# Other orders in an attention and a delta stage, and 20 transposes of the identity ahead of each head's inverse

## The reference, cut to what matters

```python
u = rmsnorm(x); p = u @ W_in                      # one projection, split by columns
o_A = neighbourhood_attention(p)                  # 8 heads of 64, a relative-position bias
o_B = gated_deltanet(p)                           # 4 heads of 128, forward and backward
o_C = rglru(p)
x = x + W_out(sum_b sigmoid(G_b(u)) * (o_b @ W_br[b]))
x = x + relu(rmsnorm(x) @ W1)**2 @ W2

# neighbourhood attention, for a block of queries and its window of keys
s = where(col_ok, q @ k.T / 8 + bias, -inf); o = softmax(s) @ v

# delta rule, for one head and direction, g summed up within a chunk
decay = exp(g_i - g_j)                            # i >= j; below strict: i > j
a_mat = (k * beta) @ k.T * strict * decay
u, w  = solve(I + a_mat, [v * beta, k * beta * exp(g)])
for each chunk:
    v_new = u - w @ S
    o = (q * exp(g)) @ S + (q @ k.T * decay) @ v_new
    S = S * exp(g_last) + (k * exp(g_last - g)).T @ v_new
o = rmsnorm(o_fwd + o_bwd) * norm_w * silu(z)
```

## Time and profile before

| | us |
|---|---|
| median of 3 runs (lowest to highest) | 3051.58 (3047.43 to 3055.48) |
| the profiled execution's own time | 3052.57 |
| span of that execution | 3050.9 |
| busy in it: PE | 2883.6 |
| DVE, ACT, POOL | 1299.3, 1072.3, 1204.7 |

### The profile page before, as it was taken

The page is one execution under the profiler, slowest core; times in us unless marked ns, Lnnn a source line. Parts: engine busy times, 40 slices in busy tenths (PEclk is TensorE's granted clock), DMA queues, the critical chain, the costliest instruction groups (busy, mean ns, idle before and its releaser), DMA issues. The chain is left out here.

```text
span 3050.9 us, 38569 instructions
## 1 busy us (share of the span) xinstructions
PE 2883.6 (95%) x15219; PEld 2351.4 (77%) x15219; DVE 1299.3 (43%) x1953; ACT 1072.3 (35%) x1829; POOL 1204.7 (39%) x805
## 2 busy tenths in 40 slices
PE   6999999999999969588778999999999999999998
PEld 5878787877888846477667887878888888888887
DVE  5233233221479959666664352322233232232323
ACT  4241313243044539455543122332332323233232
POOL 2222122121123320433422423466666676756663
PEclk9999999999999979778899999999999999999999
DMA  4434233343545357210113545332323333333331
GB/s 115 169 131 139 80 102 102 100 128 98 177 155 168 129 190 250 79 53 22 74 47 119 172 155 201 99 111 86 108 85 95 97 97 124 99 95 96 114 108 56
DMA packets 239572, 352.78 MB, mean 116 GB/s; under 512 B 32929, under 2 KB 186273, under 8 KB 239393
## 3 DMA queue, kind: packets, MB, share of 16 engines
q1 hardware_dynamic: 239392, 350.32, 35.3%
HBM read 263.71 MB, written 96.36 MB: 118 GB/s over the span
## 5 line engine op out<-in xcount | busy, mean ns | idle before, releaser
L102 PE MATMUL pj_acc<-u_hi,pj_w_hi 128*128 128x512 f32 x1464 | 576.4, 394 | 10.6 <-DVE u_lo L823 10.6
L2774 DVE TENSOR_TENSOR x_tm<-m_ps,x_tm 128x512 f32<-128x512 f32 x384 | 265.0, 691 | 744.2 <-PE m_ps L104 744.2
L104 PE MATMUL pj_acc<-u_hi,pj_w_lo 128*128 128x512 f32 x1464 | 571.8, 391 | 0.0
L103 PE MATMUL pj_acc<-u_lo,pj_w_hi 128*128 128x512 f32 x1464 | 571.2, 390 | 0.0
L551 POOL TENSOR_TENSOR pj_w_lo<-pj_w_raw,pj_w_hi 128x1024 fp32r<-128x1024 f32 x61 | 159.3, 2612 | 721.6 <-ACT pj_w_hi L600 721.6
L2656 POOL TENSOR_TENSOR m_lo<-gate,held 128x1024 fp32r<-128x1024 f32 x96 | 237.9, 2501 | 269.8 <-ACT held L2573 269.8
L102 PEld LDWEIGHTS pj_acc<-u_hi,pj_w_hi 128*128 128x128 f32 x1464 | 275.8, 188 | 85.6 <-issue 18.2
L104 PEld LDWEIGHTS pj_acc<-u_hi,pj_w_lo 128*128 128x128 f32 x1464 | 275.8, 188 | 58.2
L103 PEld LDWEIGHTS pj_acc<-u_lo,pj_w_hi 128*128 128x128 f32 x1464 | 276.1, 189 | 56.2
L102 PE MATMUL m_ps<-held 128*128 128x512 f32 x768 | 298.9, 389 | 2.4 <-DVEq L2755 2.4
L102 PE MATMUL m_ps<-held,m_h_hi 128*128 128x512 f32 x768 | 299.5, 390 | 0.0
(11 more groups left out here) (308 smaller groups left out, 4930.9 us busy)
## 6 DMA issues: line engine op xcount, KB each, us to landing
gate<-in_w_mlp_dram SPq DMA_DIRECT2D x48, 1024.0 KB, 5.4
gate<-in_w_mlp_dram SPq DMA_DIRECT2D x96, 512.0 KB, 3.7
proj<-pj_stage SPq DMA_DIRECT2D x61, 768.0 KB, 3.4
pj_w_raw<-in_w_in_dram SPq DMA_DIRECT2D x61, 512.0 KB, 5.2
gate<-proj SPq DMA_DIRECT2D x24, 768.0 KB, 4.4
mo_w_raw<-in_w_out_dram SPq DMA_DIRECT2D x48, 256.0 KB, 2.9
rpb_bias<-pj_shut SPq DMA_DIRECT2D x48, 192.0 KB, 3.0
rpb_bias<-rpb_near SPq DMA_DIRECT2D x24, 384.0 KB
```

The lines of the kernel that those rows point to most:

```text
L102: pe.matmul(out, w_hi, x_hi, start=first, stop=False)
L103: pe.matmul(out, w_hi, x_lo, start=False, stop=False)
L104: return pe.matmul(out, w_lo, x_hi, start=False, stop=last)
L2774: dve.tensor_tensor(xt, ps2[:, q % 4], xt, ALU.add).then_inc(added, 1)
```

## The change

It has these parts. Tile names are those of the code.

- Attention: SP issues bias tables 4, 5 and 6 ahead of pair 1, whose loads go in two halves at units 4 and 6; the decay rows come at unit 8 and not at 1. The columns of head 0 are not made here. Instead DVE forms -g and ln(beta) + g for all heads with two operations ahead of the loop and one in unit 6, and ACT takes the logarithm first. The 48 exponentials start at unit 14.
- Delta, arithmetic: beta goes into the exponent of the strict decays, so that `scores` is one operation of 128x512 instead of four of 128x128. The columns (`cx`) of all heads are made once, at the start, with two matmuls, eight small DVE operations and one exponential; they are gone from the inverses.
- Delta, places: the exponentials of the decay rows go from steps 0 and 2 of the inverse to steps 5 and 6 of the chunk phase before it. `cut_blocks` stands behind the state updates of its step. ACT takes over four of the copies into `dn_un`, and the inverse waits for the parts of it singly. The sum of the output stage comes behind the first U copy, its 24 length matmuls are three groups of 8 at steps 3, 4 and 5, the root at step 8 (was 5), the gate at step 15 (was 12). POOL multiplies the queries in six pieces of 512.
- Before each inverse PE transposes the identity 20 times into a PSUM bank that is free at that point.

The diff, cut to its core:

```diff
 # attention
-    DG_AT, DCOL_AT, DY_AT, DEXP_AT = 1, 6, (28, 32, 36), 8
+    DG_AT, PAIR1_AT, DCOL_AT, DY_AT, DEXP_AT = 8, (4, 6), 6, (28, 32, 36), 14
             load_bias(3)
-            for a in range(2):
-                load_qk(1, a)
-                load_v(1, a)
             for u in range(U + 4):
...
                 if n is not None:
                     load_bias(n)
+                if u in PAIR1_AT:
+                    load_qk(1, PAIR1_AT.index(u))
+                    load_v(1, PAIR1_AT.index(u))
...
                 if u == DCOL_AT:
-                    decay_columns(dve, dc, cols[:, 0], col2[:, 0], ncol2[:, 0], cx2[:, 0], gq[:, 0])
+                    dve.tensor_tensor(gbeta[:], cols[:, :, 0:2], gbeta[:], ALU.add).then_inc(d_cols, 1)
...
 # delta
-SQUARES_AT, ROOT_AT, EG_AT, CEXP_AT = 1, 5, (0, 2), 10
-LENGTHS_AT, MEAN_AT, DIAG_AT, SPREAD_AT, NORM_AT, GATE_AT = 2, 3, 5, (7, 9, 11), (8, 10, 12), 12
+SUM_AT, SQUARES_AT, LENGTHS_AT, MEAN_AT, ROOT_AT, DIAG_AT = 0, 2, (3, 4, 5), 6, 8, 8
+SPREAD_AT, NORM_AT, GATE_AT = (10, 12, 14), (11, 13, 15), 15
-COLUMNS_AT = 6
-INCL_AT = {8: 4, 11: 5, 13: 0, 15: 1}
+INCL_AT = {9: 4, 12: 5, 15: 0}
-INCL_END = {1: 3, 3: 2}
+INCL_END = {1: 1, 3: 3, 4: 2}
+WARM = 20
+EG_IN = (5, 6)
...
             def place(i):
+                for q in Q32:
+                    act.copy(by_direction(un, q, 0)[:, 0:NTB:2, :, q], compact(c1, q, 0)[:, 0:NTB:2]).then_inc(S["un0_d0"], 1)
+                act.wait_ge(S["spread"], 2 * i + 2)
...
                 pe.wait_ge(S["am_done"], i * NG6 + NG6)
                 pe.wait_ge(S["qk_done"], i * NG6 + NG6)
+                for j in range(WARM):
+                    pe.transpose(ps[:, 7, j % 4], ident[:], ident[:])
...
-                for j in range(4):
-                    last = dve.scalar_tensor_tensor(am[:, n, j], ps[:, 4 + 2 * (GRAMS.index(tg) % 2), j],
-                                                    ncol2[:, i % 2, 2 + d, 4 * tg + j:4 * tg + j + 1], decays[:, j], ALU.mult, ALU.mult)
-                last.then_inc(S["am_done"], 1)
+                dve.scalar_tensor_tensor(am[:, n], ps[:, 4 + 2 * (GRAMS.index(tg) % 2)], -1.0, decays, ALU.mult,
+                                         ALU.mult).then_inc(S["am_done"], 1)
...
-                if part == CUT_IN:
-                    cut_blocks(i)
...
+                if more and step == CUT_IN:
+                    cut_blocks(i + 1)
```

More of the change, by code:

```diff
@@ L1701, in _ @@
             act.wait_ge(mixed_landed, 16)
-            act.sem_inc(S["cexp"], 1)
             act.sem_inc(S["exp_s"], NG6)
             act.sem_inc(S["exp_i"], NG6)
+            act.wait_ge(S["columns"], 5)
+            flat_cx = cx[:].rearrange("p h a t -> p (h a t)")
+            act.activation(flat_cx, flat_cx, ACT.Exp).then_inc(S["cexp"], 1)
+            for d in range(2):
+                row_decays(0, d)
             cut_blocks(0)
@@ L1836, in main @@
                         pe.matmul(o, nb[:, j], qk2[:, i % 2, 2 * (t // 4) + d, t % 4], start=step == 0, stop=True).then_inc(S["o_mm"], 1)
+            pe.wait_ge(S["ends"], 2)
+            for d in range(2):
+                last = pe.matmul(ps[:, 3, d, 0:HEADS * NT], work[:, d * P:(d + 1) * P], cols[:, :, d], start=True, stop=True)
+            last.then_inc(S["ends"], 1)
             for x in range(NTB):
@@ L1869, in out_gate, with columns, rates @@
                 dve.scalar_tensor_tensor(oc[0], oc[0], 0.5, zt, ALU.mult, ALU.mult).then_inc(S["out_done"], 1)
[L1871 to L1875 removed]
+            def columns():
+                c = Chain(dve, S["columns"], 0, 5)
+                c.add(dve.tensor_copy(cx[:, :, 0:2], cols[:, :, 0:2]))
+                dve.wait_ge(S["ends"], 3)
+                for d in range(2):
+                    ends = ps[:, 3, d, 0:HEADS * NT].rearrange("p (h t) -> p h t", h=HEADS)
+                    c.add(dve.tensor_tensor(cx[:, :, 2 + d], ends, cols[:, :, d], ALU.subtract))
+                    c.add(dve.tensor_copy(cx[:, :, 4 + d], ends))
+                c.end()
+            def rates():
+                dve.wait_ge(S["cexp"], 1)
+                dve.scalar_tensor_tensor(cx[:, :, 0:2], cols[:, :, 2:4], -1.0, cx[:, :, 0:2], ALU.mult, ALU.mult).then_inc(S["columns"], 1)
+                dve.wait_ge(S["columns"], 6)
             def scores(i, n):
[L1879 removed]
+                tg = UN[n][0]
                 decays = am[:, n] if i else dd0[:, 2 * n]
@@ L1984, in main @@
                             out_gate(i - 1)
-                    if k == COLUMNS_AT and more:
-                        columns(i + 1, nxt)
                 dve.sem_inc(S["s0"], 1)
@@ L2005, in main @@
                         if step:
-                            dve.scalar_tensor_tensor(st[:, j], st[:, j], cx2[:, i % 2, EGL[d], t:t + 1], ps[:, j, 2], ALU.mult, ALU.add).then_inc(S["st_ev"], 1)
+                            dve.scalar_tensor_tensor(st[:, j], st[:, j], cx[:, i, EGL[d], t:t + 1], ps[:, j, 2], ALU.mult, ALU.add).then_inc(S["st_ev"], 1)
                         else:
                             dve.tensor_copy(st[:, j], ps[:, j, 2]).then_inc(S["st_ev"], 1)
+                    if more and step == CUT_IN:
+                        cut_blocks(i + 1)
                 if more:
-                    place(i + 1, False)
-                c.end()
+                    place(i + 1)
             dve.wait_ge(S["prm_in"], 16)
-            chains = [Chain(dve, S["chain"], i, K_DN) for i in range(HEADS)]
+            for d, row in ((0, P - 1), (1, 0)):
+                dve.tensor_copy(work[:, d * P:(d + 1) * P], ident[:, row:row + 1].to_broadcast([P, P])).then_inc(S["ends"], 1)
             dve.memset(ps[:, 0:2], 0.0).then_inc(S["blank"], 1)
-            dve.sem_inc(S["chain"], 8)
-            chains[0].n = 8
-            dve.sem_inc(S["cols_in"], 1)
-            for part in range(STEPS):
-                prepare(0, part, chains[0])
-            place(0, False)
+            for step in range(STEPS):
+                prepare(0, step)
+                if step == 0:
+                    columns()
+                if step == CUT_IN:
+                    cut_blocks(0)
+                if step == WIDE_IN:
+                    rates()
+            place(0)
             for i in range(HEADS - 1):
-                main(i, True, chains[i], chains[i + 1])
-            main(HEADS - 1, False, chains[HEADS - 1], None)
+                main(i, True)
+            main(HEADS - 1, False)
             dve.wait_ge(S["gated"], HEADS)
@@ L2039 @@
                 K_KEPT.append((_step, _j))
-K_DN = 1 + 7 + 1
 class MlpViews:
```

148 lines of the change are left out of this document (64 added, 84 removed).

## The result

| | before | after |
|---|---|---|
| median of 4 runs (lowest to highest), us | 3051.58 (3047.43 to 3055.48) | 3029.19 (3025.76 to 3031.12) |
| ratio, 95% interval | | 0.9924 (0.9909 to 0.9940) |
| the profiled execution's own time, its span | 3052.57, 3050.9 | 3031.12, 3029.1 |

The kernel is 22.4 us faster, where 46.6 were forecast: the sign was right and the size half. The stages tell where the rest went. The attention runs from its first score product to the start of its last product with the values, an inverse begins with its first product S, a chunk phase with its first product with `dn_un` (L1821), and what follows head 3 with the 24 length matmuls of the merge (L2355). The times are read off the two timelines of PE; the low time is worked out from the granted clock as in the prediction.

A forecast was written before the change was run, and what follows sets the result against it. The inverses, one dependent chain over PE, ACT and DVE with PE often at low clock, were taken as the bound, with waits in the attention. Terms summed to -46.9 us from 3052.6, giving 3005 for the median; range 2984 to 3034.

The forecast's parts named there:

- Start of the inverses: Start of each inverse: ACT shares copies, the sum comes later, row exponentials leave; -3.3 for heads 1 to 3, -1.5 head 0, -11.4.
- Other work inside: Inside the inverses: split lengths -4.5, columns gone less closer table loads -3.4, later gate -2.0 us.
- Chunk phases: Chunk phases: shorter scores, cut moved and earlier POOL solution, less row exponentials on ACT; -1.8 for each of three, -5.4 us.
- What bounds the kernel: Inverses are one PE, ACT, DVE chain; 92 us at low clock, at best 33 shorter (36%) at full clock.
- Attention: Attention: bias wait gone -7.9, column operations replaced -6.2, contention +2.5, exponentials over fewer units +0.5; sum -11.1 us.
- The upper figure of 15 us: Attention: by the port-lock rule, scalings beside twelve POOL masks could pay up to 15 us; the rows gave 2.5.
- Head 0's preparation: Preparation of head 0: wider scores operations -2.3, new columns work +1.2; sum -1.1 us.
- Head 0's inverse: Inverse of head 0: forecast 4.4 us shorter.
- The clock in the second halves: Second halves of the inverses: less stalling keeps the clock up longer; -5 us, bounds 0 and -20.
- rival 5: Inverses: back-to-back table loads at steps 8 and 9 drop the clock, kernel slower at 3058 us; chance 0.06.
- The transposes: Ahead of the inverses: 20 transposes keep PE from idling; -1.0 for each of three heads, -3 us; 0 to +6 by the rule.
- rival 2: Delta stages: gains hidden by POOL and ACT's fuller queue, row exponentials cost +3 a head; 3031 us, chance 0.13.

The follow-up runs named there:

- earlier_output: Also number 12: number 11 with the output stage early again (mean at step 4, root 6, spread, norm and gate pieces from 8 to 14): 3003.2 us.
- number 7: The changed kernel with SP's load order of before in the attention (pair 1 ahead of bias tables 4 to 6, decay rows at unit 1): 3029.7 us.
- numbers 8: The changed kernel with all 24 length matmuls at step 3 instead of in three groups: 3024.1 us.
- 16: earlier_output with the length matmuls in three groups at steps 3, 4, 5, the mean at 5 and the diagonal at 7: 3000.5 us.
- number 11: The changed kernel with the column matmuls behind the first Gram product, all lengths at step 3, and the gate in three pieces at steps 12, 14, 15: 3018.7 us.
- gate_pieces: The changed kernel with the gate as three pieces of 512 columns at steps 12, 14 and 15: 3025.2 us.
- number 9: The changed kernel with the decay-row exponentials of heads 1 to 3 back at steps 0 and 2 of the inverse: 3021.1 us.
- 10: The changed kernel with DVE's cut ahead of the state updates of step 2, as before: 3022.2 us.
- number 3: The kernel before with the 20 transposes, and POOL waiting for DVE's 16 copies before it multiplies the queries: 3051.8 us.
- 15: earlier_output with DVE's cut ahead of the state updates of step 2: 3004.0 us.

## Why the prediction was half right

The steps that failed are the prices of the moved work in its new places: in "Start of the inverses" the sum, in "Other work inside" the lengths and the gate (-6.5 together), and "Chunk phases" (-5.4). With the clock they were to bring most of the 28.8 us; the inverses of heads 1 to 3 gave 2.1 us, and the chunk phases became 6.9 us longer. Head 0's two stages were off by 5 us and 7 us in opposite directions.

**What bounds the kernel.** Right: the inverses are one chain over three engines, a stall stands ahead of many falls of the clock (not of all, see below), and the low time in them was there to be had. earlier_output took 40 of the 64 low us of heads 1 to 3, and its 3003 us are the time that was forecast for the change.

**Attention.** Right, -11.9 against -11.1. The bias wait went (number 7 brings 6.7 of it back) and the columns with it. Contention was under-sized: five pairs of scalings were slowed by 6.8 us together, against 2.5 in two pairs before, thus by 4.3 more and not by 2.5. The better clock (low 26 to 11 us) is what can have made up for that; no run separates it. The upper figure of 15 us that the prediction names wasn't reached.

**Head 0's preparation.** Wrong by 5 us. "The new `columns` work adds +1.2" counted the short DVE operations. The cost was in the queue of PE: its matmuls for the columns stand ahead of the Gram products and wait 6.5 us for two DVE copies, which themselves wait for the stage's first DMA. The scores were as forecast, 0.65 us each.

**Head 0's inverse.** -11.8 against -4.4. It has no output stage. With the columns' wait of 3.1 us gone and no row exponentials ahead of the S copies, PE's waits in it fell from 6.6 to 2.0 us, and the low time from 28 to 9. At 36% these 19 us are worth 7, where the share of the clock term was 1.

**Start of the inverses, and other work inside.** This is the first step that failed. I took away what the old places cost and priced the new ones too low. The wait ahead of the first product did fall, by 7.0 us in three heads; 12.9 were forecast for this start, the sum and the transposes included. But "the sum comes behind the first U copy": the step got out of the first U copy's way and into the second's, 2.4 us in each head. "At step 15 it is behind nearly all of these: -2.0": the gate is ahead of the last two U copies, 2.5 us (3.2 in head 3), and its store then holds ACT at the start of the chunk phase. "As groups of 8 they fill places where PE waits for ACT: -4.5": numbers 8 and 16 show no gain from the groups. The table loads, "+1.3" a head, were not priced too low as a wait: 2.5 us in head 1 against 2.1 before, and 0.2 against 2.1 in head 2. In all PE waited 24 us in these three inverses, and 27 before.

**The clock in the second halves.** Forecast -5 over all. The low time of the four inverses fell from 92 to 73 us, worth 7 us at 36%; but all of it is head 0's, and heads 1 to 3 stayed at 64. That the sum of this term is near its forecast is luck. In head 1's inverse the clock was low for 3.4 us each from 1350.8, 1371.3 and 1388.4, behind the waits for the sum, ACT and the U copies. A fourth fall, at 1357.7, stands behind no such wait; in heads 2 and 3 the one at the same place lasted 20.5 us, and this is most of their low time. So the stalls are one part of the reason, and the other stays open. My rival 5 named steps 8 and 9, and its price was too high by far: after it inverse 1 still ran at 0.87. That the late output stage as a whole did harm is shown by number 12 against number 11 (15.6 us, no other edit). Its parts singly (root 7.0, gate 4.0, lengths 5.1) have intervals too wide to rank them.

**Chunk phases.** This is the second step that failed: -5.4 forecast, 6.9 us longer in the three heads. Of head 1's 2.7 us, 1.2 are in the first step, where the store holds ACT, and 0.7 in the sixth, where a moved group of exponentials stands ahead of ACT's copies; 0.4 are in the fourth, which has a fall of the clock in it (5.6 us; 4.2 at full clock in gate_pieces, 5.2 before). These causes are read from the trace: no run took them back. The cut traded a wait of 2.0 us for one of 1.6, and numbers 9 and 10 show no gain from either move.

**The transposes.** The mechanism was right: they started at full clock and held it over the start of the inverse. The size isn't settled: forecast -3, measured 4.3 and 2.9 us in two pairs of kernels whose intervals overlap, and nothing in the kernel before (number 3). The rule of the Trainium skill ("TensorE: Matmul & The Clock Gate", Part 4: PE-mode transpose), that transposes don't count as PE being busy in the same way, isn't borne out by these f32 transposes: with 20 of them and 0.4 us of idle time ahead of them the second product of head 1's inverse takes 0.68 us, without them 1.12.

**Rivals.** The measured 3029 lies at rival 2 (3031), the gains hidden, and by its mechanism in part. The chunk phases took back what the wait ahead of the inverses gave, 6.9 of 7.0 us. By their first and sixth steps some 4 us of that are ACT's fuller queue, but not through the row exponentials, for which the rival charged it (number 9). The larger part is in the inverses, where new stalls stand in the place of the old ones.

**Still open.** Why the same inverse runs at 0.87 in one head and 0.74 in the next. Numbers 7, 10 and 15 show that a shift or a small edit elsewhere changes it by 3 to 10 us an inverse; no run here shows what decides it.

## What to carry to other kernels

When work is moved off one wait, look at what stands behind it in the new place, on its own engine and in the queue of the engine that takes its result, and price that as carefully as what is removed. Measure the stage behind as well: a wait that shrinks can come back as work in the next stage. Where a stage's clock depends on stalls, a single edit's time can be that of the clock in another loop: test an edit in two kernels before believing it (the cut was worth 7 us in one and 0 in the other). And an engine that gets faster can bring another engine's long operation forward beside the copies for which a third waits; a semaphore wait that costs nothing can be worth 26 us.

## What the runs showed of the hardware

- A POOL product of 3.42 us that began 0.3 us before 16 small DVE copies would have ended made these take 8.07 us instead of 4.86, and the kernel 26 us slower; one wait on POOL took all of it back (3078.0 to 3051.8).
- Beside POOL's products of 128x512, the DVE sum of 128x1536 took 2.37 us in one piece (1.76 in the kernel before, where it began 0.2 us ahead of POOL's product) and 1.29 + 1.77 + 1.76 us in three pieces.
- 20 transposes of the identity took 2.37 us at full clock and kept it there; ahead of head 0's inverse, where they began after 8.4 us of idle time, they took 4.30:

```profile
1251.32 4.30 PE L1749 MATMUL dn_ps<-ident 128*128 128x128 f32 x20 [8.42 <-DVE dn_qk L1904]
```

- The same 600 matmuls of an inverse took 42 to 55 us in the variants, with a granted clock of 0.68 to 0.96.
